# Block 2's mixers without fences, the next stage's first scores ahead, and unread identity products in the differential attentions

## What is computed

```python
def token_mixer_2(h, w_in, w_out, lam_params, subln_gain, layer):
    proj = h @ w_in
    ...
    o_a = dilated_attention(to_heads_2(qa, N_HEADS_DIL) * (HEAD_DIM_2 ** -0.5), to_heads_2(ka, N_HEADS_DIL), to_heads_2(va, N_HEADS_DIL))
    ...
    o_b = differential_attention(qb[:, :, 0], qb[:, :, 1], kb[:, :, 0], kb[:, :, 1], to_heads_2(vb, N_HEADS_DIFF), lam.astype(jnp.float32))
    o_b = rmsnorm(o_b, subln_gain) * (1.0 - lam_init)
    o_c = stick_breaking_attention(to_heads_2(qc, N_HEADS_SB) * (HEAD_DIM_2 ** -0.5), to_heads_2(kc, N_HEADS_SB), to_heads_2(vc, N_HEADS_SB))
    mixed = jnp.concatenate([from_heads(o_a), from_heads(o_b), from_heads(o_c)], axis=-1).astype(h.dtype)
    return mixed @ w_out
```

## Time and profile before

| | before |
|---|---|
| median of three runs | 3589.32 us (3571.4 to 3592.34) |
| profiled execution | 3566.98 us |
| its span | 3565.2 us |
| TensorE busy | 3207.4 us (90%) |
| VectorE busy | 1925.5 us (54%) |
| ScalarE busy | 1255.2 us (35%) |
| mean granted TensorE clock | 0.943 of 2.4 GHz |

### The profile page before, as it was taken

One profiled execution on the slowest core, in us unless ns is written; L12 is line 12 of the kernel. 1 busy time (PEld: TensorE's weight loads), 2 busy tenths in 40 slices (PEclk: granted clock), 3 DMA queues, 4 the chain that ended last, 5 costly groups with the idle time before them and its releaser, 6 DMA issues.

```text
span 3565.2 us, 61054 instructions
## 1 busy us (share of the span) xinstructions
PE 3207.4 (90%) x26580; PEld 2556.1 (72%) x26580; DVE 1925.5 (54%) x2834; ACT 1255.2 (35%) x2066; POOL 172.3 (5%) x167
## 2 busy tenths in 40 slices
PE   6988778889798887799999699999999999799999
PEld 5866667775443333699888468998899887469997
DVE  3356665555321112887332648873886333658863
ACT  3226432321100000454332655443544323654432
POOL 0003222130100000000000000000000000000000
PEclk8989898888899999899999799999999999799999
DMA  6140000014599997233330012333233331012322
GB/s 245 55 147 16 3 3 3 3 35 178 225 396 421 421 421 315 67 106 117 111 132 27 34 59 71 107 105 121 72 107 115 110 113 60 1 59 88 106 98 83
DMA packets 174020, 441.50 MB, mean 124 GB/s; under 512 B 5954, under 2 KB 97852, under 8 KB 149180
## 3 DMA queue, kind: packets, MB, share of 16 engines
q1 hardware_dynamic: 173756, 437.61, 33.1%
HBM read 435.49 MB, written 2.10 MB: 123 GB/s over the span
## 4 chain that ended last, share of the span: by engine, by line
PE 67%; DVE 9%; DMA 7%; ACT 3%; issue 3%; SPq 0%; POOL 0%; DVEq 0%; ACTq 0%; POOLq 0%
PE banks L338 8%; PE banks L3091 7%; PE banks L3094 7%; PE banks L3093 7%; PE banks L2263 5%; PE banks L3212 4%; PE banks L3213 4%; PE banks L3211 4%; DMA arena<-in_exp_w_down 4%; DMA arena<-in_exp_w_up 3%; PE banks L1466 1%; PE banks L378 1%; PE banks L334 1%; PE banks L782 1%; PE banks L1489 1%
## 5 line engine op out<-in xcount | busy, mean ns | idle before, releaser
L2263 PE MATMUL banks<-ring,arena 128*64 128x512 f32 x1120 | 264.3, 614 | 41.9 <-DMA ring<-in_exp_w_gate 18.2
L3213 PE MATMUL banks<-tail_r,hid_r 128*128 128x512 f32 x704 | 279.9, 398 | 0.0
L3212 PE MATMUL banks<-ring_r,two_r 128*128 128x512 f32 x640 | 254.2, 397 | 0.0
L3211 PE MATMUL banks<-tail_r,two_r 128*128 128x512 f32 x640 | 250.8, 392 | 0.0
L2263 PEld LDWEIGHTS banks<-ring,arena 128*64 128x64 f32 x1120 | 90.9, 141 | 201.9 <-issue 183.6
L3091 PE MATMUL banks<-ring_r,tail_r 128*128 128x256 f32 x624 | 175.8, 282 | 9.0 <-DVE arena L3176 9.0
L295 DVE TENSOR_TENSOR hid_r<-arena,two_r 128x1024 fp32r<-128x1024 f32 x40 | 49.0, 1226 | 238.1 <-ACT two_r L292 223.8
L3093 PE MATMUL banks<-ring_r,tail_r 128*128 128x256 f32 x624 | 176.2, 282 | 0.0
L3091 PE MATMUL banks<-mix_r,tail_r 128*128 128x256 f32 x624 | 175.7, 282 | 0.0
L3093 PE MATMUL banks<-h_r,tail_r 128*128 128x256 f32 x624 | 175.0, 280 | 0.0
L3094 PE MATMUL banks<-mix_r,ring_r 128*128 128x256 f32 x608 | 171.4, 282 | 0.0
(11 more groups left out here) (538 smaller groups left out, 8830.4 us busy)
## 6 DMA issues: line engine op xcount, KB each, us to landing
ring<-in_exp_w_gate SPq DMA_DIRECT2D x31, 2048.0 KB, 17.1
ring<-in_w_ffn_gate SPq DMA_DIRECT2D x44, 1024.0 KB, 5.4
ring<-in_w_ffn_up SPq DMA_DIRECT2D x44, 1024.0 KB, 5.4
ring<-in_exp_w_down SPq DMA_DIRECT2D x20, 2048.0 KB, 17.6
ring<-in_w_ffn_down SPq DMA_DIRECT2D x20, 2048.0 KB, 7.8
ring<-in_exp_w_up SPq DMA_DIRECT2D x19, 2048.0 KB, 16.1
ring<-in_w_in SPq DMA_DIRECT2D x17, 2048.0 KB, 11.2
arena<-in_exp_w_up SPq DMA_DIRECT2D x13, 2048.0 KB, 17.6
```

Source lines behind the costliest of these rows:

```text
L2263: ins = TE.matmul(banks[64 * e:64 * e + 64, b0 + hf, :], lhs(kk, e), w[:, k, hf * 512:(hf + 1) * 512], start=(kk == 0), stop=(kk == KD - 1))
L3211: TE.matmul(bank, h_hi, w_hi[:, c, ns], start=(f == 0), stop=False)
L3212: TE.matmul(bank, h_hi, w_lo[:, c, ns], start=False, stop=False)
L3213: ins = TE.matmul(bank, h_lo, w_hi[:, c, ns], start=False, stop=(f == NF - 1))
```

## The change

Attentions of the mixers get `ahead_of` (what is issued before this stage's last transposes on TensorE, and before the last evacuations on ScalarE) and `prior` (the waits on single results of the stage before, which take the place of the fence). So: the dilated attention's scores of steps 0 and 1 run behind group 28 of the projection; group 30 is now read by ScalarE, and group 31 by ScalarE inside the dilated attention, after the exponentials of units 0 and 1; its weights lie in the ring slot of the fifth projection load instead of the arena. The differential attention's step 0 runs before the dilated one's last transposes. `z(0)` and its Softplus run before the differential attention's last transposes and last evacuation. In every step of the differential attentions (`nset == 2`) TensorE multiplies the identity by itself three times before it waits for the normalised weights, and three times more before the values of the step before; the results are overwritten by the transposes and read by nobody. The products for the norm move behind `after_sums(0)`, and the squares and "sub_var" with them. Output tiles (0, 0) and (0, 1) run before the values of heads 4 and 5, and the splits for parts 0 and 1 move earlier or into the stick stage. Stick and output stage have no fence. On SyncE the two loads of w_out change places with the load of the differential bias. The first block's attention uses the same function without `prior`, and its order is unchanged.

```diff
+                        if "behind" in g:
+                            g["behind"](l)
...
+                    scores(l, 0)
+                    if ahead == 4:
+                        scores(l, 1)
+                def f_pe(l):
+                    if not prior:
+                        first_scores(l)
+                    def unread(k):
+                        b, c = tb_of[k, 0]
                         if nset == 1:
...
+                            return
+                        if c >= 3:
+                            l.wait_ge(*past(name, "T", *by_cnt[c - 3]))
+                        elif prior and k == 0:
+                            prior["turn"](l)
+                        for i in range(3):
+                            TE.matmul(banks[:, b, 0:P], ident, ident, start=True, stop=True)
                     def turn(k):
+                        unread(k)
                         for v in range(2):
                             l.wait_ge(*past(name, "P", 2 * k + v))
+                        if prior and k == 0:
+                            prior["turn"](l)
...
+                            scores(l, k)
                         if bias is None and 1 <= k <= N:
...
+                        if 2 <= k <= N:
+                            unread(k - 1)
...
+                        if k == N and ahead_of:
+                            ahead_of(l)
                         if bias is not None and 1 <= k <= N:
                             turn(k - 1)
                 def f_dve(l):
+                    if prior:
+                        prior["dve"](l)
                     def inverse(u):
...
+                            if k == N + 1 and ahead_of:
+                                ahead_of(l)
...
+                            if k == 0 and prior:
+                                prior["act"](l)
...
+                            if prior and u == 2:
+                                prior["act"](l)
...
+                yield first_scores, lambda l: out_(l, N - 1)
+                stage(name, fence=prior is None, pe=f_pe, act=f_act, dve=f_dve, pool=pool_fn)
...
+                    def z(l, i):
+                        if i >= 2:
+                            l.wait_ge(*past(nb, "clamped", i - 2))
+                        elif i:
+                            l.wait_ge(*past(nm + "dif", "T", 7, 1))
+                        else:
+                            l.wait_ge(*past(nm + "dif", "max", 15))
+                        for s_ in (0, 1, 3, 2):
...
+                        if i >= 2:
+                            l.wait_ge(*past(nb, "zc", i - 2))
+                        else:
+                            l.wait_ge(*past(nm + "dif", "turned", 6 + i, 1))
+                        l.did(S.activation(sp[:, i % 2, :], flat(i), ACT.Softplus).then_inc(l.sem, 1), nb, "ln", i)
+                    def stick_begin(l):
+                        if l is act:
+                            softplus(l, 0)
+                        else:
+                            z(l, 0)
+                    def last_value_rows(l):
+                        l.wait_ge(*past(nm, "made", 31))
+                        gs[31]["read"](l, banks[:, 7, :])
+                        l.name_last(nm, "read", 31)
+                    def first_dil(l, u):
+                        l.wait_ge(*past(nm, "read", 24 + u))
+                    def turn_dil(l):
...
+                        for i in (28, 29, 30):
+                            l.wait_ge(*past(nm, "read", i))
...
+                                    ahead_of=stick_begin,
+                                    prior={"bank": lambda l, u: l.wait_ge(*past(di, "max", 21 + 2 * u)),
+                                           "turn": lambda l: l.wait_ge(*past(di, "T", 11, 1)),
+                                           "values": lambda l: l.wait_ge(*past(di, "out", 2)),
+                                           "dve": lambda l: l.wait_ge(*past(di, "biased", 23)),
+                                           "evac": lambda l, k: l.wait_ge(*past(di, "pv", 10 + k)),
+                                           "act": lambda l: dil_last(l)})
+                    dif_scores, _ = next(dif)
...
+                    sb_at = ws[4][0][0] % RING * SLOT
+                    dil = attention(di, ((0, 1), (2, 3), (4, 5)), width, s_dil, lambda h, j: vt[:, j, h * HD:(h + 1) * HD],
+                                    lambda pair: [(mixT[:, pair[0] // 2, :], slice(0, P))], HD ** -0.5,
+                                    ([region(sb_at + i * T, T) for i in range(6)], pt, stats[:, 64:112].rearrange("p (a b) -> p a b", b=8)),
+                                    bias=lambda h, t: b_dil[h][:, 384 - P * t:T], need=(nm + "bias",), ahead_of=dif_scores,
+                                    prior={"bank": first_dil, "turn": turn_dil,
+                                           "values": lambda l: l.wait_ge(*past(nm, "read", 31)),
+                                           "dve": lambda l: None, "evac": lambda l, k: None, "act": last_value_rows})
+                    dil_scores, dil_last = next(dil)
...
+                    gs[28]["behind"] = dil_scores
+                    gs[30]["by"], gs[31]["by"] = "act", None
+                    products(nm, gs, units=units, fence=False, presplit=1, begun=(2, early))
+                    small(nm + "bias2", [(b_dif, a["k_bias"][6:10, :, 0:T].rearrange("h p n -> p h n"))], after=nm)
+                    next(dil, None)
+                    slot_user[ws[4][0][0] % RING] = (di, "turned", 11, 1)
+                    next(dif, None)
...
-                        z(0)
-                        l.wait_ge(*past(nb, "squares"))
-                        for k in range(2):
-                            ins = TE.matmul(banks[:, 6 + k, :], ones2, sq2[:, k, :], start=True, stop=True)
-                        l.did(ins.then_inc(l.sem, 1), nb, "sub_sums")
-                        z(1)
+                        z(l, 1)
                         for i in range(6):
                             after_sums(i)
+                            if i == 5:
+                                l.wait_ge(*past(on, "lo", 0))
+                                l.wait_ge(*past(on + "m", "lo", 0))
+                                l.wait_ge(*past(nb, "clamped", 4))
+                                tile(0, 0)
                             if i:
                                 values(i - 1)
+                            else:
+                                l.wait_ge(*past(nb, "squares"))
+                                for k in range(2):
+                                    ins = TE.matmul(banks[:, 6 + k, :], ones2, sq2[:, k, :], start=True, stop=True)
+                                l.did(ins.then_inc(l.sem, 1), nb, "sub_sums")
                             if i + 2 < 6:
-                                z(i + 2)
+                                z(l, i + 2)
+                        l.wait_ge(*past(nb, "clamped", 5))
+                        tile(0, 1)
                         values(5)
...
-                            if i == 4:
+                            if i == 3:
                                 split(l, on, 0, w_units[0], KD)
                                 split(l, on + "m", 0, m_units[0], KD)
+                        l.wait_ge(*past(nb, "scaled"))
+                        split(l, on + "m", 1, m_units[1], KD)
+                        split(l, on, 1, w_units[1], KD)
                         l.wait_ge(*past(nb, "pv", 5))
                         out_copy(l, 5)
...
-                        l.did(V.tensor_tensor(sq2, mixT[:, 3:5, :], mixT[:, 3:5, :], ALU.mult).then_inc(l.sem, 1), nb, "squares")
...
-                            if i == 5:
-                                split(l, on, 0, w_units[0], KD)
-                                split(l, on + "m", 0, m_units[0], KD)
                             if i == 0:
+                                l.wait_ge(*past(df, "out", 1))
+                                l.did(V.tensor_tensor(sq2, mixT[:, 3:5, :], mixT[:, 3:5, :], ALU.mult).then_inc(l.sem, 1), nb, "squares")
+                            if i == 1:
                                 l.wait_ge(*past(nb, "sub_sums"))
                                 l.did(V.tensor_scalar(sq2, banks[:, 6:8, :], 1.0 / HD, NORM_EPS, ALU.mult, ALU.add).then_inc(l.sem, 1),
                                       nb, "sub_var")
@@ -3482,33 +3582,44 @@
                                 if h >= 2:
                                     l.wait_ge(*past(nb, "pv", h - 2))
                                 l.did(V.tensor_scalar(wt[:, h % 2, :], flat(h), 0.0, None, ALU.min).then_inc(l.sem, 1), nb, "clamped", h)
+                                if h == 3:
+                                    split(l, on, 0, w_units[0], KD)
+                                if h == 4:
+                                    split(l, on + "m", 0, m_units[0], KD)
                                 l.wait_ge(*past(nb, "exp", h))
                                 mask(wt[:, h % 2, :])
```

(1 more changed line is left out.)

165 lines of the change are left out of this document (84 added, 81 removed).

## The result

The changed kernel takes 3547.76 us (median of ten runs, 3536.36 to 3556.68) where the kernel before, beside it on the same chip, takes 3571.46 us (ten runs, 3559.64 to 3592.34). The ratio is 0.9926 with a 95% interval of 0.9905 to 0.9947; on a later chip it was 0.9925 (0.9899 to 0.9951). Of 3589.3 us that is 26.6 us, with 19 to 34 as the interval. I had forecast 25. So the sum came out right; its terms did not all come out right, and that is what the rest is about.

What follows compares the result with a forecast made beforehand. Bounds: VectorE in the dilated attention, TensorE in the stick stage, nobody saturated in the differential. 3.3 + 2.3 + 4.0 - 1.6 + 5.1 - 0.5 = 12.6 us a mixer, 25 in all: 3564 us median, range 3540 to 3583.

Steps and rivals of the forecast that it cites:

- part 5: Leaving the stick stage: two output tiles fill waits before the last two heads' values, splits earlier; 5.1 us a mixer gained.
- the price of the clock: Stick stage: the new wait before the third score product may lower the clock; 0.5 us a mixer, up to 1.7.
- part 4: Entering the stick stage: first score product moves ahead, but the third starts later; 1.6 us a mixer lost.
- Part 1: Entering the dilated attention: scores moved under the projection's last groups start the fifth unit earlier; 3.3 us a mixer.
- Part 2: Dilated to differential attention: first two units' scores precede the last transposes, third unit starts earlier; 2.3 us a mixer.
- Part 3: Differential attention: identity products raise clock and shorten VectorE's six waits for scores; 4.0 us a mixer, bounds -0.5 and 6.4.
- the clock stays down: Differential attention: identity products fail to raise the clock and give nothing; whole gain 17 us, 3572 us; chance 0.25.
- products in the way: Differential attention: clock stays at half and every identity group stands on the path; 2.4 us slower, 3592; chance 0.05.

## Why the prediction was right, and where it was not

The total was right and the mechanism of its largest doubt, the clock in the differential attention, was right. Parts 1 to 3 were a little too small. Three terms were well off: part 5 and the price of the clock came out worse than forecast by 3 to 5 and by 2.8 us a mixer, part 4 better by about 2. Taken together they were too large: by the marks the gain is 17 us and not 25.

1. **Part 1**, 3.3 us a mixer: the fifth unit came 6.01 us after the mark and comes 1.47 after it; less 0.93 for the moved scores, 3.6. Right. The run of it alone was not made.
2. **Part 2**, 2.3 us. From the last dilated values to the last but one differential ones the first mixer took 49.7 us before, 47.0 without the products, 42.1 changed: 2.7 us for this part. Right. In the second mixer the same difference is only 1.1.
3. **Part 3**, 4.0 us inside the stage: 4.8 and 5.2 (none against three, stretch A). Right in size, in place, and in its mechanism, clock up and six waits from 9.3 to 4.4. Two inputs were wrong and did no harm: a product costs over twice what I had from the transposes of the earlier trace rows, and TensorE's waits took them all the same. What I missed is the larger half, 7.8 and 8.1 us in stretch B, because I had the clock of one stage end with the stage.
4. **The rival "the clock stays down"** fails on this. I gave it a gain of 17 us, by leaving out part 3. The run without the products is that case: it gains nothing that can be measured (ratio 0.9993), and by the marks it is 2.3 and 4.6 us a mixer slower than the kernel before. It would have been 3587, not 3572, and so was the nearest rival to a loss; my rival for a loss, products in the way, was far off, and needed a stage without waits, as the dilated attention then showed.
5. **Part 4**, a loss of 1.6 us from a third score product that starts later: it starts 0.1 and 0.6 us earlier than before, so the step was wrong; what stretch B lost is all clock (see 6). The wait is 2.7 us, as forecast (2.9). What failed is the entry: I had the second score product 1.2 us earlier, or 1.8 at full clock, and it is 3.0 and 3.5 us earlier (7.3 and 6.8 us behind the mark between A and B, where it was 10.3). I took the attention's tail to be 2.5 us longer by table load and Softplus, while the load was over before the first score product began, the Softplus ran under identity products and transposes, and TensorE's wait for the last evacuation stayed what it was (0.83 us, before 0.78). The run with the stick stage's head in place says the same from the other side: its second score product too is 6.8 us behind the mark.
6. **The price of the clock** for that wait, 0.5, at most 1.7: much too small. From the third to the fourth score product there are 11.65 us in both mixers and were 8.33, so it is 3.3 us, all that B lost and more; in the runs that have the wait it is 1.7 to 5.0 us (10.0 us in the second mixer of the run with late splits, 13.3 in that of the run with one product). I had let the behaviour after the 1.58 us wait weigh as much as that after the 2.91 us one, though the new wait is nearly as long as the latter; and in the kernel before with the products the clock fell behind the wait of 1.58 us as well.
7. **Part 5**, 5.1 us: 0.1 and 1.8. Of the steps that failed this is the largest. From the start of the sixth score product on it is right: to the last output product there were 67.6 us before and are 62.7 with the splits late, 4.9 us less, and the first tile follows the last cumulative products with no wait (3133.91 and 3134.05 in the second mixer). But I looked only at VectorE for what the splits' new place does ("no longer standing ahead of head 4's clamp"), and costed ScalarE's half of them, 2.9 us one head earlier, at nothing. There they stand ahead of table load, Softplus, mask, sums and the clamp of head 3, and TensorE waits 1.44 us for that. The price was 4.8 and 3.1 us: 1.5 for the wait and the rest for the clock behind it. And of the 4.9 us the tiles themselves are only 1.2 or 1.3, as the run with the tiles in place shows.
8. **The sum.** By the marks 8.7 and 10.4 us a mixer, less 0.9 each for the moved scores: 17 us against 25 forecast. The spans of the two profiles say 20, the medians 23.7, the ratio 26.6. The profile of the kernel before was one of its quicker executions, and I cannot tell from one trace of each how much of the other 6 to 9 us lies in the mixers. By the marks it was 7.7 and 9.5 us a mixer, not 12.6, so that the total came out as forecast is partly luck.

ScalarE's table loads again have the function behind them with no idle time (2068.08 and 2069.37), so the trace keeps disagreeing with the drain of about 1.38 us that the Trainium skill gives in "ScalarE: Activation LUTs", section "What ACT_TABLE_LOAD costs".

## What to carry to other kernels

Cost a wait on TensorE at what follows it, not at its length: here one of 2.7 us cost 6, one of 1.4 us cost 1.5 where the clock stayed up and 3 to 5 where it fell, and both were made by an instruction queued ahead of a clamp that did not need it. Price the clock across the end of a stage, since the next stage starts at what the last one left. Unread products are good filler where TensorE waits longer than they take (11.6 us of them at full clock into a stage where TensorE had 20 us without work) and a loss where it does not (17.7 into 8): that sum can be made from the profile before.

## What was not expected of the hardware

An unread 128x128 product of the identity takes 0.26 us at full clock and 0.53 at half, while a transpose of the same shape takes 0.13 (eight in 1.04 us). The same instructions, with one product a group, ran at 0.70 in one mixer and 0.56 in the other of one execution, 192 and 204 us, and behind the same wait of 1.4 us the clock fell in one mixer and not in the other: one profile of such a kernel does not tell how it behaves. And with the clock at 1.00 throughout in place of 0.89 the differential attention became no shorter (42.7 and 42.1 us up to its last but one values).
